# ScalarE's order within a chunk: evictions and side work ahead of the rounding of the chunk three ahead

## The chip, the cores and the metric

One NeuronCore of a Trainium2 chip runs the whole program. The metric is the device time of one execution in microseconds (us), less is better. The engines are TensorE (PE, its weight loads PEld), VectorE (DVE), ScalarE (ACT), GpSimd (POOL) and SyncE (SP), which issues nearly all DMAs. Each runs its own instructions in order and waits on semaphores for the others.

## The reference, cut to what matters

The reference chains two transformer blocks over 256 tokens of width 2048, all in float32. Nearly all its arithmetic is `x @ w` with a token matrix of 256 rows:

```python
# block 1
shift, scale, gate = split(silu(c) @ w_ada + b_ada, 3)        # and the same for the context
h = rmsnorm(x) * (1 + scale) + shift;   p = h @ w_in          # 2048 x 9216
attn = attention(rope(norm(q)), [k, kc], [v, vc])             # 12 query heads, 4 key heads
y = (sigmoid(g_a) * ((attn * silu(z_a)) @ w_proj_a)
     + sigmoid(g_b) * ((fourier_mix(u_b) * silu(z_b)) @ w_proj_b)) @ w_out
x = rmsnorm(x + gate * y) * final_g
# block 2
u = rms(x) * (1 + scale1) + shift1;     proj = u @ w_in_2     # 2048 x 18432
o_a = stick_breaking_attention(q, k, v)                       # 16 heads
o_b = gated_delta_rule(conv(q), conv(k), conv(v), g, beta)    # 16 heads, chunks
x = x + gate1 * ((sigmoid(ga) * (o_a @ p_a) + sigmoid(gb) * (o_b @ p_b)) @ w_out_2)
x = x + gate2 * ((silu(u2 @ w_gate) * (u2 @ w_up)) @ w_down)  # u2 from x as u, width 5632
```

## The kernel before, in words

**Stripes and chunks.** Every large weight matrix is read once, in stripes of 512 output columns. A stripe is a series of chunks; a chunk is 256 rows of weights (two tiles of 128x512, 512 KB) and is loaded by one DMA into a ring `raw` of six slots. There are 936 chunks in one fixed order, `of_chunk`; a chunk's number is called its beat. The phases come in the order ada with ctx and the first of in1 between, in1, ab1, out1, in2, pb2, ab2, out2, ffa, dna, ffb, dnb.

**Two roundings.** A float32 product is made of three passes in the format fp32r. For chunk n, ScalarE writes the rounded weights `w_hi` (`split_hi`, L411), then VectorE writes the rest `w_lo = raw - w_hi` (`split_lo`, L421). Both have three slots (`HL = 3`). TensorE then does eight matmuls of 128x512 on `w_hi` (L675) and four on `w_lo` (L681); in the ada phase it is two and two with a 4 column operand (L661, L665). Eight ada chunks need no rounding. The slot of chunk n + 3 is free when TensorE is done with chunk n, so both roundings of n + 3 wait for that. VectorE's `split_lo(n + 3)` also waits for ScalarE's `split_hi(n + 3)`.

**One beat of each engine.** Everything that isn't the stream of chunks is a side task, cut into steps by generators (`Track`, `yield k` gives the beat of the next step). TensorE at beat b: the matmuls of chunk b, then its side steps of b. VectorE at beat b: what the end of a stripe asks for, its side steps, `split_lo(b + 3)`, then a part of a matrix-vector product by hand (`macc`, L710). ScalarE at beat b: `split_hi(b + 3)`, then what the end of a stripe asks for, then its side steps. SP at beat b: the load of chunk b + 6 (after both roundings of chunk b), the load for L710, the store of a stripe that ended three beats earlier, its side steps. At two beats (starts of in2 and ffa) a hook follows: the normalisation of the rows.

**What ScalarE does at the end of a stripe.** A "store" stripe: it copies one half of the result from PSUM to `ost` (L560; VectorE the other half, L580), after an earlier store from that buffer has landed. A "rows" stripe (out1, out2): `square_rows`, sums of squares (L473, L480) of what VectorE's `add_rows` (L455, L458, L460 or L462) has just written. A "gate" stripe: a sigmoid. An "ada" stripe: the copy of a 4x512 row (L864), for which TensorE's L872 waits one beat later.

**Side steps of ScalarE that the text speaks of.** `first_squares` (L998), `stage_act` (L854) and `prep_act` (L899) at the start; squares of the attention heads (L1190) and the copy L1216; `gdn_act` (L1648, L1665, L1668, L1688 and others); `ba_act` (L1396); `sb_act` (three steps in one beat, L1971, L1973, L1975, for which VectorE's L1937 waits two beats later); `merge_sig_act` (L753), which waits for a DMA. TensorE's side steps that wait: L872, L523 (transposes of the normalised rows, behind VectorE's L508), L1556 (behind VectorE's L1753), L2007 (behind ScalarE's L1978) and L2015 (behind VectorE's L1950).

Of the kernel before, what the change touches and what calls it, by code (L numbers as in the profile page):

```python
# [49 lines left out]
HL = 3  # L50
# [87 lines left out]
def program(nc, a, y_out, dram):  # L138
    ctx = ExitStack()
    with ctx:  # L140
# [152 lines left out]
        def plain(st, kc):  # L293

            return st.phase == "ada" and kc == 4
        P0 = len(of_chunk)
        of_chunk += whole(S[3:])
        CHUNKS = len(of_chunk)
# [15 lines left out]
        def wait(eng, sem, value):  # L314
            if value > 0:
                eng.wait_ge(sem, value)
# [25 lines left out]
        for j, (base, step) in enumerate(mod_from):  # L342
            base = max(base, max(sum_at, default=-1) + 1)
            for k in range(MC):
                beat = base + (3 * step * (k // 2)) // 2 + k % 2
# [53 lines left out]
        def split_slot(n):  # L399

            k = halved[n]
            return k % HL, last_in[k - HL] + 1 if k >= HL else 0

        def split_hi(act, n):
            if plain(*of_chunk[n]):
                return
            use, slot = divmod(n, RAW)
            to, before = split_slot(n)
            act.wait_ge(s[f"raw{slot}"], 16 * (use + 1))
            wait(act, s["pe"], before)  # L410
            nc.scalar.copy(w_hi[:, to], raw[:, slot]).then_inc(s["hi"], 1)  # L411
# [23 lines left out]
        def evac(eng, st, m, copy, sem):  # L435

            eng.wait_ge(s["pe"], st.end)
            staging(eng, st)
            copy(ost[:, st.slot, m], bank(st.bank + m)).then_inc(s[sem], 1)
# [24 lines left out]
        def square_rows(act, st):  # L464

            cols = slice(st.o * W, (st.o + 1) * W)
            k = st.res - 1
            if st.phase == "out1":
                act.wait_ge(s["res_x"], st.res)
                for m in range(M):  # L470

                    wait(act, s["sq"], 4 * k + m)
                    nc.scalar.activation(sq_junk, ost[:, st.slot, m], ACT.Square,  # L473
                                         accum_out=nss[:, 0, m, st.o:st.o + 1]).then_inc(s["sq"], 1)
            if st.phase != "dnb":
                act.wait_ge(s["res"], st.res)
                done = 4 * k + 2 if st.phase == "out1" else 16 + 2 * (k - 4)
                for m in range(M):
                    act.wait_ge(s["sq"], done + m)
                    nc.scalar.activation(sq_junk, E[:, m, cols], ACT.Square,  # L480
                                         accum_out=nss[:, 1, m, st.o:st.o + 1]).then_inc(s["sq"], 1)
# [68 lines left out]
        def stream_act(act, items, hooks):  # L550
            sides = [Track(act, l) for l in items]
            for n in range(HL):
                split_hi(act, n)
            for beat in range(CHUNKS):
                if beat + HL < CHUNKS:
                    split_hi(act, beat + HL)
                st = ends.get(beat)
                if st is not None:
                    if st.kind == "store":
                        evac(act, st, 0, lambda dst, src: nc.scalar.copy(dst, src), "ev_act")  # L560
                    elif st.kind == "rows":
                        square_rows(act, st)
                    elif st.kind == "gate":
                        ff_gate_act(act, st)
                    elif st.kind == "ada":
                        ada_row_act(act, st)
                for side in sides:
                    side.run(beat)
                if beat + 1 in hooks:
                    hooks[beat + 1](act)  # L570

# [142 lines left out]
        def ff_gate_act(act, st):  # L714
            act.wait_ge(s["pe"], st.end)

            wait(act, s["ff_ev"], 2 * st.f)
            nc.scalar.activation(ff_sig, pair(st.bank), ACT.Sigmoid).then_inc(s["ff_sig"], 1)
# [142 lines left out]
        def ada_row_act(act, st):  # L861
            act.wait_ge(s["pe"], st.end)
            wait(act, s["ad_col"], st.idx - 1)
            nc.scalar.copy(ada_row[:, st.idx % 2], ada_out(st.idx)).then_inc(s["ad_row"], 1)  # L864
# [1236 lines left out]
        def _(act):  # L2101
# [55 lines left out]
            items += [(FFB, norm_rest, 1), (FFB + 5, h2_stored, 0)]  # L2157
            turns = [(st.n0, merge_sig_act, st) for st in MERGES] + [(st.done + 1, ep_act, st) for st in TURNS]
            stream_act(act, [first, preps, gates, items, sorted(turns, key=lambda item: item[0])], {B: norm_x1, FFB: norm_h2})

        @block.vector
# [211 lines left out]
```

## Time and profile before

| | |
|---|---|
| runs | 2927.20, 2916.00, 2926.41 us, median 2926.41 |
| profiled execution, its own time | 2926.73 us |
| its span, first to last instruction | 2924.8 us (1.9 us lie around it) |
| PE busy | 2838.9 us, 97% |
| PEld busy | 2328.3 us, 80% |
| DVE busy | 2024.5 us, 69% |
| ACT busy | 1348.3 us, 46% |
| DMA | 709.71 MB, mean 243 GB/s |
| mean granted TensorE clock | 0.987 |

How to read it: a row of a timeline is start, duration, engine and line, operation, output<-inputs, shapes, count; in brackets the idle time of the engine just before and what ended it. A row without brackets followed its predecessor without idle time. TensorE's granted clock has two levels, 1.2 GHz (0.5) and 2.4 GHz (1.0).

### The profile page before, as it was taken

What the parts mean: (1) busy time and instruction counts of PE and PEld (TensorE: products, weight loads), DVE (VectorE), ACT (ScalarE), POOL (GpSimd) and SP (SyncE); (2) the same over time, 40 slices, a digit from 0 to 9 for tenths busy, and PEclk for the clock granted to TensorE, in tenths of its full rate; (3) what the DMA queues carried; (4) which work ended last, traced back from release to release, by engine and by line L of the source; (5) the groups of instructions that cost most, each with busy time, mean ns of one, the idle gap of its engine ahead of it and who ended that gap; (6) DMA issues with size and microseconds to landing.
All of it is one profiled execution on the core that took longest, in us unless ns stands there. A gap on an engine that the chain in (4) does not pass through costs nothing.

```text
span 2924.8 us, 37083 instructions
## 1 busy us (share of the span) xinstructions
PE 2838.9 (97%) x13703; PEld 2328.3 (80%) x13703; DVE 2024.5 (69%) x2413; ACT 1348.3 (46%) x1725; POOL 73.3 (3%) x49
## 2 busy tenths in 40 slices
PE   7899999999989999999999999999999999999999
PEld 3468888778777888888888788887878888888877
DVE  6678777768776777777775788775657765445554
ACT  6544444444463535354544555554454444444433
POOL 0000000000000101000000000000000000000000
PEclk9999999999999999999999999999999999999999
DMA  8888777869758665656556788877757775665664
GB/s 311 283 321 325 259 251 240 278 219 343 279 207 318 208 217 181 216 169 218 173 180 233 266 288 295 307 251 251 254 192 257 281 249 190 214 201 190 197 243 151
DMA packets 223475, 709.71 MB, mean 243 GB/s; under 512 B 26768, under 2 KB 42432, under 8 KB 220480
## 3 DMA queue, kind: packets, MB, share of 16 engines
q1 hardware_dynamic: 222144, 703.04, 69.5%
q0 software_dynamic: 576, 4.19, 0.3%
q8 instruction: 109, 1.79, 0.3%
q14 instruction: 70, 0.57, 0.1%
q10 hardware_dynamic: 576, 0.11, 0.0%
HBM read 663.20 MB, written 44.06 MB: 242 GB/s over the span
## 4 chain that ended last, share of the span: by engine, by line
PE 86%; DVE 5%; DMA 3%; issue 3%; ACT 2%; POOL 1%; SPq 0%; DVEq 0%; ACTq 0%
PE ps L675 48%; PE ps L681 24%; DVE w_lo L421 2%; PE ps L1602 1%; PE ps L1592 1%; DMA mraw<-in_w_mod 1%; DVE macc L710 1%; ACT w_hi L411 1%; PE ps L1256 1%; PE ps L1241 1%; PE ps L1596 1%; PE ps L788 1%; DMA E<-in_ctx 1%; POOL arena L1819 1%; PE ps L665 0%
## 5 line engine op out<-in xcount | busy, mean ns | idle before, releaser
L411 ACT CAST w_hi<-raw 128x1024 fp32r<-128x1024 f32 x928 | 971.2, 1049 | 1443.4 <-PE ps L681 1397.7
L421 DVE TENSOR_TENSOR w_lo<-raw,w_hi 128x1024 fp32r<-128x1024 f32 x928 | 1127.6, 1221 | 548.9 <-ACT w_hi L411 544.9
L675 PE MATMUL ps<-w_hi,hT_hi 128*128 128x512 f32 x2688 | 749.1, 401 | 8.3 <-ACT w_hi L411 5.4
L681 PE MATMUL ps<-w_lo,hT_hi 128*128 128x512 f32 x2688 | 721.4, 390 | 5.7 <-DVE w_lo L421 5.7
L675 PE MATMUL ps<-w_hi,hT_lo 128*128 128x512 f32 x2688 | 721.6, 390 | 0.0
L681 PEld LDWEIGHTS ps<-w_lo,hT_hi 128*128 128x128 f32 x2688 | 505.6, 188 | 113.4 <-DVE w_lo L421 7.4
L675 PEld LDWEIGHTS ps<-w_hi,hT_lo 128*128 128x128 f32 x2688 | 506.4, 188 | 107.6
L675 PEld LDWEIGHTS ps<-w_hi,hT_hi 128*128 128x128 f32 x2688 | 490.9, 189 | 106.5 <-issue 14.4
L710 DVE SCALAR_TENSOR_TENSOR macc<-mraw,silu_c,macc 128x512 f32<-128x512 f32 x420 | 314.5, 749 | 20.0 <-DMA mraw<-in_w_mod 12.1
L681 PE MATMUL ps<-w_lo,fT_hi 128*128 128x512 f32 x800 | 215.3, 391 | 3.7 <-DVE w_lo L421 3.7
L675 PE MATMUL ps<-w_hi,fT_hi 128*128 128x512 f32 x800 | 217.9, 394 | 0.0
L675 PE MATMUL ps<-w_hi,fT_lo 128*128 128x512 f32 x800 | 215.6, 392 | 0.0
L681 PEld LDWEIGHTS ps<-w_lo,fT_hi 128*128 128x128 f32 x800 | 151.2, 189 | 35.8 <-DVE w_lo L421 4.2
L675 PEld LDWEIGHTS ps<-w_hi,fT_lo 128*128 128x128 f32 x800 | 151.3, 189 | 31.9
L675 PEld LDWEIGHTS ps<-w_hi,fT_hi 128*128 128x128 f32 x800 | 149.2, 189 | 30.3
L580 DVE COPY ost<-ps 128x512 f32<-128x512 f32 x64 | 44.0, 687 | 27.0 <-PE ps L681 21.3
L1719 DVE SCALAR_TENSOR_TENSOR arena<-ps,arena 128x255 f32<-128x255 f32 (+2 forms) x144 | 59.1, 471 | 0.2 <-ACT arena L1640 0.2
L1795 DVE TENSOR_TENSOR arena<-arena,ps 128x1024 f32<-128x1024 f32 x24 | 29.3, 1221 | 40.0 <-PE ps L1602 40.0
L661 PE MATMUL ps<-w_hi,sT 128*4 128x512 f32 x112 | 40.0, 442 | 9.7 <-ACT w_hi L411 9.7
L1592 PEld LDWEIGHTS ps<-arena 128*128 128x128 f32 x384 | 46.5, 191 | 1.9
L1602 PEld LDWEIGHTS ps<-arena 128*128 128x128 f32 x384 | 46.5, 191 | 1.9
L665 PE MATMUL ps<-w_lo,sT 128*4 128x512 f32 x112 | 39.0, 433 | 8.1 <-DVE w_lo L421 7.4
(300 smaller groups left out, 1779.5 us busy)
## 6 DMA issues: line engine op xcount, KB each, us to landing
raw<-in_w_in SPq DMA_DIRECT2D x432, 512.0 KB, 4.7
mraw<-in_w_mod SPq DMA_DIRECT2D x192, 512.0 KB, 4.2
raw<-in_w_gate SPq DMA_DIRECT2D x88, 512.0 KB, 4.2
raw<-in_w_up SPq DMA_DIRECT2D x88, 512.0 KB, 4.3
raw<-in_w_down SPq DMA_DIRECT2D x88, 512.0 KB, 4.3
raw<-in_w_ada SPq DMA_DIRECT2D x64, 512.0 KB, 5.5
raw<-in_w_out SPq DMA_DIRECT2D x64, 512.0 KB, 4.5
scratch_p<-ost SPq DMA_DIRECT2D x54, 512.0 KB, 5.3
```

Source lines behind the costliest of these rows:

```text
L411: nc.scalar.copy(w_hi[:, to], raw[:, slot]).then_inc(s["hi"], 1)
L421: nc.vector.tensor_tensor(w_lo[:, to], raw[:, slot], w_hi[:, to].bitcast(F32), ALU.subtract).then_inc(s["lo"], 1)
L580: evac(dve, st, 1, lambda dst, src: nc.vector.tensor_copy(dst, src), "ev_dve")
L661: pe.matmul(ada_out(st.idx), sT[:, kc * CK + t], w_hi[:, slot, t], start=(kc == 0 and t == 0), stop=False)
L665: mm = pe.matmul(ada_out(st.idx), sT[:, kc * CK + t], w_lo[:, slot, t], start=False, stop=(kc == st.chunks - 1 and t == CK - 1))
L675: pe.matmul(bank(st.bank + m), x, w_hi[:, slot, t], start=(kc == 0 and t == 0 and xp == 0), stop=False)
L681: mm = pe.matmul(bank(st.bank + m), x, w_lo[:, slot, t], start=False, stop=(kc == st.chunks - 1 and t == CK - 1))
L710: ins = nc.vector.scalar_tensor_tensor(macc[:], mraw[:, mk % 2, t], col, macc[:], ALU.mult, ALU.add)
L1592: mm = pe.matmul(tiles(4)[:, t], gL[:, t], gXT[:, t], start=True, stop=True)
L1602: mm = pe.matmul(tiles(4)[:, t], gX[:, t], gR[:, t], start=True, stop=True)
L1719: ins = vec.scalar_tensor_tensor(y, x, cw[:, k, h, 3 - j:4 - j], y, ALU.mult, ALU.add)
L1795: GV.done(vec.tensor_tensor(gXT, gXT, tiles(4), ALU.subtract), f"xt{lv}")
```

## The change

ScalarE's `split_hi(beat + HL)` is issued behind the stripe's end work and the side steps of the beat, ahead of the hook, no longer at the head of the beat. The instructions are the same ones, and no other engine's order is touched.

```diff
             for beat in range(CHUNKS):
-                if beat + HL < CHUNKS:
-                    split_hi(act, beat + HL)
                 st = ends.get(beat)
                 if st is not None:
                     if st.kind == "store":
...
                         ada_row_act(act, st)
                 for side in sides:
                     side.run(beat)
+                if beat + HL < CHUNKS:
+                    split_hi(act, beat + HL)
                 if beat + 1 in hooks:
                     hooks[beat + 1](act)
```

## Rows read from the trace of the kernel before

**Rows 1.** The page, section 1 (busy us, share of the span, instructions) and section 5.

```profile
PE 2838.9 (97%) x13703; PEld 2328.3 (80%) x13703; DVE 2024.5 (69%) x2413; ACT 1348.3 (46%) x1725; POOL 73.3 (3%) x49
...
L411 ACT CAST w_hi<-raw 128x1024 fp32r<-128x1024 f32 x928 | 971.2, 1049 | 1443.4 <-PE ps L681 1397.7
```

**Rows 2.** Waits of TensorE: for whom, us in total, times, longest.

```profile
PE ps L872 <- ACT aff L864: 15.1, 6, 4.7
...
PE ps L523 <- DVE E L508: 14.3, 2, 8.2
...
PE ps L1556 <- DVE arena L1753: 3.4, 4, 1.3
```

**Rows 3.** Timeline, one plain beat of ScalarE and VectorE.

```profile
836.39 1.05 ACT L411 CAST w_hi<-raw 128x1024 fp32r<-128x1024 f32 x1 [1.67 <-PE ps L681]
...
837.47 1.23 DVE L421 TENSOR_TENSOR w_lo<-raw,w_hi 128x1024 fp32r<-128x1024 f32 x1 [1.49 <-ACT w_hi L411]
```

**Rows 4.** Timeline of the ada phase, one row copy.

```profile
132.19 0.63 PE L665 MATMUL ps<-w_lo,sT 128*4 128x512 f32 x2
...
134.63 1.04 ACT L411 CAST w_hi<-raw 128x1024 fp32r<-128x1024 f32 x1 [2.47 <-DMA raw<-in_w_ada]
...
135.58 0.57 ACT L864 COPY aff<-ps 4x512 f32<-4x512 f32 x1
...
136.40 1.83 PE L872 MATMUL ps<-stat,aff 4*128 4x2 f32 x8 [3.58 <-ACT aff L864]
```

**Rows 5.** Timeline of the ada phase, one preparation of operands.

```profile
96.15 1.22 DVE L421 TENSOR_TENSOR w_lo<-raw,w_hi 128x1024 fp32r<-128x1024 f32 x1
...
96.27 1.14 ACT L899 CAST hT_hi<-arena 128x512 fp32r<-128x512 f32 x2 [0.34 <-DVE arena L889]
```

**Rows 6.** Timeline of the delta rule's first turn.

```profile
998.59 1.06 ACT L1648 ACTIVATE arena<-arena 128x1024 f32<-128x1024 f32 x1
...
999.68 1.23 DVE L1725 TENSOR_TENSOR arena<-arena 128x1024 f32<-128x1024 f32 x1 [2.45 <-ACT arena L1648]
...
1010.62 1.06 PE L1556 MATMUL ps<-c_ident,arena 128*128 128x128 f32 x8 [1.31 <-DVE arena L1753]
```

**Rows 7.** Timeline at the normalisation that opens in2.

```profile
842.72 1.22 DVE L421 TENSOR_TENSOR w_lo<-raw,w_hi 128x1024 fp32r<-128x1024 f32 x1
...
844.65 0.17 DVE L487 TENSOR_REDUCE nms<-nss 128x4 f32<-128x16 f32 x1 [0.71 <-ACT aff L480]
```

**Rows 8.** Timeline at the end of out1's third stripe.

```profile
816.85 1.05 ACT L411 CAST w_hi<-raw 128x1024 fp32r<-128x1024 f32 x1 [1.67 <-PE ps L681]
...
822.04 1.07 PE L675 MATMUL ps<-w_hi,hT_hi 128*128 128x512 f32 x4
...
823.27 2.94 ACT L411 CAST w_hi<-raw 128x1024 fp32r<-128x1024 f32 x3
```

**Rows 9.** Waits of ScalarE for DMAs: us in total, times, longest.

```profile
ACT E L753 <- DMA E<-scratch_p: 5.5, 1, 5.5
...
ACT b_two L1396 <- DMA arena<-in_w_ba: 5.4, 1, 5.4
...
ACT ost L560 <- DMA scratch_pc<-ost: 4.4, 1, 4.4
```

**Rows 10.** Timeline of TensorE at the start of ab2.

```profile
2001.60 2.05 PE L675 MATMUL ps<-w_hi,hT_hi 128*128 128x512 f32 x4 [2.80 <-ACT w_hi L411]
```

**Rows 11.** Stretch (us): busy PE, PEld, DVE, ACT, POOL; granted clock; DMA share; GB/s.

```profile
1990.00:2010.00 20.00, 17.20 (x69) 13.80 (x68) 8.19 (x7) 9.14 (x8) 0.00 (x0) 0.91 0.72 254
```

**Rows 12.** Timeline of a stick-breaking turn, ScalarE and VectorE.

```profile
1810.27 0.85 ACT L1971 ACTIVATE arena<-arena 128x768 f32<-128x768 f32 x1
...
1812.78 1.03 ACT L411 CAST w_hi<-raw 128x1024 fp32r<-128x1024 f32 x1
...
1813.85 1.22 DVE L421 TENSOR_TENSOR w_lo<-raw,w_hi 128x1024 fp32r<-128x1024 f32 x1 [2.47 <-ACT w_hi L411]
...
1816.44 0.95 DVE L1937 SCALAR_TENSOR_TENSOR arena<-arena 128x768 f32<-128x768 f32 x1
```

## Prediction

> **What bounds the kernel now.** I read the page first. TensorE is busy for 2838.9 of 2924.8 us, while the rounding on ScalarE leaves 1443.4 us of idle time in front of its 928 instances [rows 1]. So TensorE sets the time, and the change can win only from the 86 us in which TensorE stands still. The view of TensorE's waits says on what it stands: 15.1 us in six waits on the row copy L864, 14.3 us in two waits on the row normalisation, 3.4 us in four waits on VectorE's L1753, and smaller ones [rows 2]. No line of it names L560 or L580, the evictions. A stripe's banks are wanted again eight chunks later.
>
> Then the timelines. In a plain beat ScalarE is idle for 1.67 us until TensorE is done with chunk b, rounds chunk b + 3 in 1.05 us, and VectorE follows with 1.23 us [rows 3]. TensorE needs the rounded chunk only after two more chunks: rounding started at 816.85, its first matmul at 822.04 [rows 8]. That is 5.19 us, of which 4.14 us are slack (the rest is the rounding itself). This slack is the cover of the change. It hides any side task on ScalarE below about 4 us, and does not hide those that wait longer, nor those where VectorE's next task is itself on the path. For VectorE rounds chunk b + 3 behind ScalarE, in order, and all its later work stands behind that.
>
> **The change, part by part.** Nothing is added or removed; 928 roundings of 1.05 us move behind the side work of their beat. Two things follow. (a) Side work no longer waits for the raw chunk's DMA or for TensorE's chunk b, and starts 0.95 to 2.7 us earlier where its own inputs are there. (b) The rounding of b + 3, and with it VectorE's rounding and its next side task, wait for whatever ScalarE's side work waits for. SP's loads wait for both roundings of a chunk three beats old and have room; ScalarE issues no DMA in these beats.
>
> *Evictions.* 64 copies start 0.95 us earlier, worth 0: no wait of TensorE names them [rows 2]. The Trainium skill (PSUM — Partial Sum Buffer, Summary: rules for kernel authors) says to evacuate promptly, as the space is tight; by that rule the evictions alone would bring time, by the rows nothing.
>
> *Row copies in the ada phase (gain).* TensorE was done with chunk 60 at 132.8 (132.19 + 0.63), but the rounding ahead of the copy waited for a DMA until 134.63, and the copy came at 135.58; TensorE stood for 3.58 us [rows 4]. The copy now comes at 132.2, so about 3.5 us go. The same working on the other waits on L864 gives 2.1, 1.2, 0.5 and 1.8, and 0 for the first, where ScalarE itself is late. Together 9.1; the bounds are 2 (loads become the limit: DMA engines were 83% busy there) and 11.
>
> *Preparation of operands in the ada phase (loss).* L899 waits for VectorE (0.34 us idle before 96.27) and ends at 97.4; VectorE rounded at 96.15 [rows 5]. The rounding by ScalarE now ends at 98.4, so VectorE is held for 2.2 us on a stretch where it is the bound. Three such: 1.7 + 2.2 + 2.2 = 6.1; bounds 2 and 8. The fourth lies under full-length chunks and is hidden.
>
> *Attention turns and Fourier part (gain).* Squares L1190 and the copy L1216 start up to 2.7 us earlier; the small stalls of TensorE that hang on them sum to 2.3. Bounds 0 and 3.
>
> *Delta rule (gain).* L1648 stood behind the rounding, and VectorE idled for 2.45 us for it; TensorE later waited 1.31 us for the end of that chain [rows 6]. L1648's inputs are there one beat earlier, so VectorE gains more than 1.3 us, and all four waits (3.4 us [rows 2]) go. Bounds 0 and 3.4. In the solver's beats ScalarE's copy waits for TensorE, but there the side matmuls lengthen the slack to some 10 us: 0.
>
> *Normalisation, twice (loss).* VectorE rounded at 842.72 while ScalarE summed squares, and its statistics began when the squares were done, at 844.65 [rows 7]. Now ScalarE rounds only from 844.6 to 845.7, VectorE rounds behind it until 846.9, and the statistics begin 2.25 us later, with TensorE waiting for them already. Two places: 4.5. Bounds 4 and 6.
>
> *out1 (loss).* In the third stripe's last beat the squares of ScalarE ended at 823.3, and TensorE wanted the chunk at 822.04 [rows 8]. The rounding now ends at 824.4: 2.4 us of a stall that wasn't there. The second stripe gives 1.4 by the same sum. The first ends in a DMA delay; there the rounding would move from 769.2 behind squares that end at 777.5, and TensorE's twelve matmuls cost 3.5 more after its present stall. Sum 7.3; bounds 3 and 11.
>
> *Waits for DMAs on ScalarE (loss).* L753 waited 5.5 us at the start of ab2, L560 4.4 us once, L1396 5.4 us [rows 9]. Behind the first, TensorE already stalled for 2.80 us [rows 10]; one more chunk is now behind it, 2.8 us. Behind the second the slack of 4.14 is spent: 1.6. Behind the third VectorE is held, but earlier work there came 1.35 sooner: 0.9. Sum 5.3; bounds 2 and 9.
>
> *Stick-breaking turns (loss, the largest).* L1971, L1973 and L1975 follow one another from 1810.27 to 1812.8, all in one beat, and start when VectorE's input is there, not because of the rounding. After them ScalarE rounded for the next beat, and VectorE, idle for 2.47 us, rounded at 1813.85 and reached L1937 2.59 us later [rows 12]. Now two roundings stand behind L1975, ending 1813.85 and 1814.9; VectorE's second one begins at 1815.1, and L1937 at 1817.7 instead of 1816.44: 1.3 us, on a chain without idle time up to TensorE's next side matmuls. The same rows of the eight turns give 2.3, 0.9, 0, 0.8, 1.3, 0.7, 0, 0: 6.0. Bounds 0 (VectorE's other work gives way) and 10.
>
> *The first turn's start* gains 0.5, attention's first, with a table load, loses 0.3.
>
> *TensorE's clock.* After the stall at 2001.60 four matmuls took 2.05 us instead of 1.07 [rows 8, 10], and the granted clock of that stretch was 0.91 on average [rows 11]: part of it ran at 1.2 GHz. A stretch at that level costs about 1.6 us. New stalls of 2 us and more (out1, stick-breaking, the stored copy) buy some, the vanished ones of the ada phase give some back: +3, bounds -2 and +8.
>
> *Sum:* gains 9.1 + 2.3 + 3.4 + 0.5 = 15.3; losses 6.1 + 4.5 + 7.3 + 5.3 + 6.0 + 0.3 = 29.5; clock 3. Net +17.2 on 2926.7 of the profiled execution, which lies 0.3 above the median of 2926.4: 2943.6 and, against the median, 2943.
>
> **The skill's rule on waits.** The rows say that 15.1 us of TensorE's idle time are put down to ScalarE's row copy [rows 2]. The Trainium skill (Perfetto Trace Analysis, Optimization Strategies) says that when the matmul engine waits for other engines, the work that blocks the path is to be made faster. By it the change is right and the time some 15 us shorter; it counts what ScalarE hands to TensorE sooner, not the hand-over that is put off in exchange.
>
> **The rivals.**
>
> *The gains alone stay (faster).* The place is VectorE: if it has other work to do while its rounding is held, and TensorE's slack of 4.14 us covers the rest, only the gains remain: 2926.4 - 15.3 = 2911. It decides at the point where held-up work is below 4.14 us everywhere. For it: 69% of VectorE is busy, so there is other work. Against it: its queue is in order, so other work can't step in, and five places exceed the slack in the rows above.
>
> *Both cancel (no change).* The stick-breaking chain and the ada preparations are estimates from two engines' order. If VectorE catches up before TensorE's side matmuls (-6), and the DMA waits fall out shorter than in the one profiled execution (-3), the sum is +8: 2934.
>
> *Held loads (much slower).* Where the rounding is held for 8 us (out1's first stripe, ab2) the slots of `raw` come free later, SP waits in order, and the load of the by-hand product and of the next chunks bunch behind one another. Each of the two would cost another 5 to 10 us, with more time at 1.2 GHz: 2958. For it: that place already is a DMA delay. Against it: slots of `raw` are freed by chunks three beats older, which are long rounded.
>
> **Chances.** The forecast (slower, around 2943) 0.52; both cancel 0.34; faster 0.04; held loads 0.10. What a measurement can tell from no change is about 0.5%, 14.6 us: slower means above 2941. Of the forecast's 0.52 some 0.10 fall below that bound, so slower gets 0.42 + 0.10 = 0.52; within gets 0.34 + 0.10 = 0.44; faster 0.04. The range of 8 in 10 runs from 2928 (most of "both cancel") to 2958.
>
> **What would show it right or wrong.** In the profile of the changed kernel TensorE's waits on L864 should fall from 15.1 to about 6, and those on L1753 vanish. The waits on VectorE's L508 should grow from 14.3 to about 19. New waits of TensorE on w_hi should stand in out1, near the start of ab2 and near 200 us; those on L1950 and L1978 should grow by about 6 in the stick-breaking turns. ScalarE's idle time in front of L753, L473 and L1971 should stand ahead of the rounding. The prediction is wrong if TensorE's waits don't grow in sum by some 14 us, if VectorE rounds in the normalisation beat before the statistics without idling, or if the time changes by more than 35 us, which no row here would explain.

## The result and the profile after

The changed kernel took 2952.35 us (median of 4 runs, 2945.91 to 2953.07), the kernel before on the same chip 2924.56 us (4 runs). The ratio is 1.0099, with a 95% interval from 1.0083 to 1.0116: 29 us more (24 to 34). The prediction was 2943, with 2928 to 2958 as its range. Direction and range were right; the loss is 12 us larger than the sum said.

The page of the changed kernel, sections 1 and 5 (its span is 2951.1 us, before 2924.8):

```profile
PE 2844.8 (96%) x13703; PEld 2327.6 (79%) x13703; DVE 2026.4 (69%) x2413; ACT 1345.2 (46%) x1725; POOL 80.2 (3%) x49
...
L411 ACT CAST w_hi<-raw 128x1024 fp32r<-128x1024 f32 x928 | 967.8, 1049 | 953.3 <-PE ps L681 918.2
```

ScalarE's idle time ahead of the rounding fell from 1443.4 us [rows 1] to 953.3, since part of its waiting now stands ahead of other work. The span is 26.3 us longer. Of that, 5.9 us are busy time of TensorE with the same 13703 instructions (2844.8 less 2838.9), which goes with a mean granted clock of 0.983 where it was 0.987, and 20.4 us are idle time (106.3 less 85.9). In the changed kernel the eviction L560 is L558.

The waits of TensorE: for whom, us in total, times, longest. After:

```profile
PE ps L675 <- ACT w_hi L411: 23.5, 6, 12.2
PE ps L523 <- DVE E L508: 18.5, 2, 10.2
PE ps L661 <- ACT w_hi L411: 16.1, 7, 6.5
PE ps L665 <- DVE w_lo L421: 14.1, 18, 1.8
PE ps L2007 <- ACT arena L1978: 6.5, 4, 2.0
PE ps L690 <- DVE macc L710: 4.4, 2, 2.8
...
PE ps L681 <- DVE w_lo L421: 3.2, 5, 2.4
...
PE ps L872 <- ACT aff L864: 2.0, 1, 2.0
...
PE ps L1556 <- DVE arena L1725: 0.8, 3, 0.3
```

And the rows of before for the same matmuls that weren't shown above:

```profile
PE ps L661 <- ACT w_hi L411: 9.7, 3, 6.5
PE ps L681 <- DVE w_lo L421: 9.4, 5, 4.4
PE ps L665 <- DVE w_lo L421: 7.4, 8, 1.7
PE ps L675 <- ACT w_hi L411: 5.4, 2, 2.8
...
PE ps L2007 <- ACT arena L1978: 2.3, 2, 1.4
```

The exchange can be read line by line. The waits on the row copy fell from 15.1 us [rows 2] to 2.0 and those on L1753 are gone (0.8 us on L1725 stand in their place). The waits on rounded chunks grew: L675 by 18.1, L661 by 6.4, L665 by 6.7 us; only those of L681 on the rest `w_lo` fell, by 6.2; 4.4 of these are one wait in out1 that went into the 12.2 us of L675. The two normalisations took 4.2 us more (14.3 [rows 2] to 18.5), the exponential L1978 4.2.

Where the time came in, as the difference (after less before) of the starts of the same chunk's first matmul (below: the chunks' shift). The last column is the same step in those kernels of the experiments below that leave the stretch as it was (8 to 10 for each row):

| at (time before) | what lies behind it | after less before, us | step | step where nothing was changed |
|---|---|---|---|---|
| 169 | ada phase | +3.5 | +3.5 | -4.9 to +1.9 |
| 607 | in1, attention, Fourier part | +2.5 | -1.0 | -0.6 to +1.8 |
| 855 | ab1, out1, first normalisation | +16.1 | +13.6 | -1.2 to +1.4 |
| 911 | start of in2 | +19.0 | +2.9 | -2.7 to +0.3 |
| 1616 | delta rule | +16.3 | -2.7 | 0.0 |
| 1643 | start of the first stick-breaking turn | +14.1 | -2.2 | -1.5 to +0.1 |
| 1960 | eight stick-breaking turns | +26.4 | +12.3 | 0.0 to +0.8 |
| 2187 | ab2, out2, second normalisation | +28.6 | +2.2 | -4.6 to +0.1 |
| 2916 | feed-forward part | +26.3 | -2.3 | -2.4 to +0.1 |

So two profiles show what out1, the delta rule and the stick-breaking turns cost or give, and say little of the ada phase and of ab2. The last step isn't the change's: it is a wait at 2839 us, 3.75 us before and 2.39 after, with the clock behind it, which shrank by as much in experiments that leave this part alone (2.50 in one, 2.31 in another). Now the places, with the rows of after that answer to those of before.

*Row copy and preparation in the ada phase* (answers to [rows 4, 5]):

```profile
98.46 1.14 ACT L899 CAST fT_hi<-mraw 128x512 fp32r<-128x512 f32 x2 [1.74 <-DVE mraw L889]
...
103.00 1.23 DVE L421 TENSOR_TENSOR w_lo<-raw,w_hi 128x1024 fp32r<-128x1024 f32 x1 [2.15 <-ACT w_hi L411]
...
138.82 1.05 PE L872 MATMUL ps<-stat,aff 4*128 4x2 f32 x8
```

The matmul behind the row copy starts without idle time, where it had waited 3.58 us. In exchange ScalarE waits 1.74 us for VectorE's L889 with its rounding behind it, and VectorE then waits 2.15 us for that rounding: the two engines take turns waiting for one another.

*out1 and the first normalisation* (answers to [rows 7, 8]):

```profile
782.43 2.04 PE L675 MATMUL ps<-w_hi,hT_hi 128*128 128x512 f32 x4 [12.16 <-ACT w_hi L411]
...
832.58 2.93 ACT L411 CAST w_hi<-raw 128x1024 fp32r<-128x1024 f32 x3
...
833.75 1.17 PE L675 MATMUL ps<-w_hi,hT_hi 128*128 128x512 f32 x4 [2.68 <-ACT w_hi L411]
...
857.37 1.23 DVE L421 TENSOR_TENSOR w_lo<-raw,w_hi 128x1024 fp32r<-128x1024 f32 x1 [2.79 <-ACT w_hi L411]
858.51 0.16 DVE L487 TENSOR_REDUCE nms<-nss 128x4 f32<-128x16 f32 x1
...
861.03 3.68 PE L523 MATMUL ps<-c_ident,E 128*128 128x128 f32 x16 [10.22 <-DVE E L508]
```

In the third stripe the three roundings stand in one block behind the squares, and TensorE waits 2.68 us where it had waited for nothing. At the normalisation VectorE's rounding stands right ahead of the statistics L487: they wait for it, and it waited 2.79 us for ScalarE's rounding, which now stands behind the squares. TensorE's wait L523 grew from 8.15 to 10.22 us.

*A stick-breaking turn*, the one of [rows 12]:

```profile
1835.58 0.85 ACT L1975 ACTIVATE arena<-arena 128x768 f32<-128x768 f32 x1
1836.33 2.94 ACT L411 CAST w_hi<-raw 128x1024 fp32r<-128x1024 f32 x3
...
1837.39 2.36 DVE L421 TENSOR_TENSOR w_lo<-raw,w_hi 128x1024 fp32r<-128x1024 f32 x2 [3.60 <-ACT w_hi L411]
...
1841.12 0.95 DVE L1937 SCALAR_TENSOR_TENSOR arena<-arena 128x768 f32<-128x768 f32 x1
...
1847.48 0.84 ACT L1978 ACTIVATE arena<-arena 128x768 f32<-128x768 f32 x1 [5.89 <-DVE arena L1947]
...
1848.38 0.87 PE L2007 MATMUL ps<-c_ident,arena 128*128 128x128 f32 x6 [1.98 <-ACT arena L1978]
```

From the end of ScalarE's three steps (1835.58 + 0.85) to L1937 it is now 4.69 us; before it was 3.56 us (1812.88 to 1816.44). VectorE's idle time ahead of its rounding grew from 2.47 to 3.60.

### The profile page after: what moved, and what is told of

Read it like the earlier page. It is cut to its first block, busy times and chain, and to the rows that moved or that the text cites. A ratio compares the mean times of both kernels' runs of the same rounds, so it can differ in the third digit from the quotient of the medians.

```text
span 2951.1 us, 37082 instructions
## 1 busy us (share of the span) xinstructions
PE 2844.8 (96%) x13703; PEld 2327.6 (79%) x13703; DVE 2026.4 (69%) x2413; ACT 1345.2 (46%) x1725; POOL 80.2 (3%) x49
## 3 DMA queue, kind: packets, MB, share of 16 engines
q8 instruction: 109, 1.79, 0.2%
## 4 chain that ended last, share of the span: by engine, by line
PE 84%; DVE 6%; issue 3%; ACT 3%; DMA 3%; SPq 0%; POOL 0%; DVEq 0%; ACTq 0%
PE ps L675 48%; PE ps L681 24%; DVE w_lo L421 2%; PE ps L1592 1%; PE ps L1602 1%; ACT w_hi L411 1%; DVE macc L710 1%; DVE arena L1719 1%; PE ps L1256 1%; PE ps L1241 1%; DMA mraw<-in_w_mod 1%; PE ps L1596 1%; PE ps L788 1%; DMA raw<-in_w_ada 1%; PE ps L690 0%
## 5 line engine op out<-in xcount | busy, mean ns | idle before, releaser
L411 ACT CAST w_hi<-raw 128x1024 fp32r<-128x1024 f32 x928 | 967.8, 1049 | 953.3 <-PE ps L681 918.2
L675 PE MATMUL ps<-w_hi,hT_hi 128*128 128x512 f32 x2688 | 751.0, 401 | 25.6 <-ACT w_hi L411 23.5
L681 PE MATMUL ps<-w_lo,hT_hi 128*128 128x512 f32 x2688 | 721.6, 390 | 0.8 <-DVE w_lo L421 0.8
L675 PE MATMUL ps<-w_hi,hT_lo 128*128 128x512 f32 x2688 | 721.7, 390 | 0.0
L675 PEld LDWEIGHTS ps<-w_hi,hT_lo 128*128 128x128 f32 x2688 | 506.6, 188 | 107.8
L681 PEld LDWEIGHTS ps<-w_lo,hT_hi 128*128 128x128 f32 x2688 | 505.9, 188 | 108.6 <-DVE w_lo L421 2.5
L675 PEld LDWEIGHTS ps<-w_hi,hT_hi 128*128 128x128 f32 x2688 | 490.9, 189 | 126.2 <-issue 29.3
L710 DVE SCALAR_TENSOR_TENSOR macc<-mraw,silu_c,macc 128x512 f32<-128x512 f32 x420 | 314.5, 749 | 21.2 <-DMA mraw<-in_w_mod 13.1
L675 PE MATMUL ps<-w_hi,fT_hi 128*128 128x512 f32 x800 | 219.1, 396 | 0.0
L681 PE MATMUL ps<-w_lo,fT_hi 128*128 128x512 f32 x800 | 215.1, 391 | 2.4 <-DVE w_lo L421 2.4
L675 PE MATMUL ps<-w_hi,fT_lo 128*128 128x512 f32 x800 | 216.1, 392 | 0.0
L681 PEld LDWEIGHTS ps<-w_lo,fT_hi 128*128 128x128 f32 x800 | 150.8, 189 | 34.4 <-DVE w_lo L421 2.8
L675 PEld LDWEIGHTS ps<-w_hi,fT_lo 128*128 128x128 f32 x800 | 151.9, 190 | 32.2
L675 PEld LDWEIGHTS ps<-w_hi,fT_hi 128*128 128x128 f32 x800 | 149.9, 190 | 31.0 <-issue 0.6
L558 ACT COPY ost<-ps 128x512 f32<-128x512 f32 x64 | 37.6, 587 | 97.4 <-PE ps L681 90.7
L1688 ACT COPY arena<-ps 128x1024 f32<-128x1024 f32 x20 | 20.4, 1019 | 118.4 <-PE ps L1596 118.4
L661 PE MATMUL ps<-w_hi,sT 128*4 128x512 f32 x112 | 39.2, 434 | 16.1 <-ACT w_hi L411 16.1
L665 PE MATMUL ps<-w_lo,sT 128*4 128x512 f32 x112 | 39.5, 438 | 14.7 <-DVE w_lo L421 14.1
L1602 PEld LDWEIGHTS ps<-arena 128*128 128x128 f32 x384 | 46.5, 191 | 1.9
```

The costliest lines, as they stand in the source:

```text
L661: pe.matmul(ada_out(st.idx), sT[:, kc * CK + t], w_hi[:, slot, t], start=(kc == 0 and t == 0), stop=False)
L665: mm = pe.matmul(ada_out(st.idx), sT[:, kc * CK + t], w_lo[:, slot, t], start=False, stop=(kc == st.chunks - 1 and t == CK - 1))
L675: pe.matmul(bank(st.bank + m), x, w_hi[:, slot, t], start=(kc == 0 and t == 0 and xp == 0), stop=False)
L681: mm = pe.matmul(bank(st.bank + m), x, w_lo[:, slot, t], start=False, stop=(kc == st.chunks - 1 and t == CK - 1))
L710: ins = nc.vector.scalar_tensor_tensor(macc[:], mraw[:, mk % 2, t], col, macc[:], ALU.mult, ALU.add)
L1602: mm = pe.matmul(tiles(4)[:, t], gX[:, t], gR[:, t], start=True, stop=True)
```

## The experiments

All use one edit of the kernel before, which puts the rounding in one of three places of ScalarE's beat. `at` is 0 for the head (as before), 1 for behind the stripe's end work, 2 for behind everything (as in the change); the experiments differ in the line that sets it.

```diff
             for beat in range(CHUNKS):
-                if beat + HL < CHUNKS:
+                at = ...
+                if beat + HL < CHUNKS and at == 0:
                     split_hi(act, beat + HL)
...
+                if beat + HL < CHUNKS and at == 1:
+                    split_hi(act, beat + HL)
                 for side in sides:
                     side.run(beat)
+                if beat + HL < CHUNKS and at == 2:
+                    split_hi(act, beat + HL)
```

The theory was that the loss is made in a few beats, in which ScalarE waits with a rounding queued behind it and either TensorE lacks the chunk or VectorE is held behind its own rounding. The rival was a loss spread over all beats, evictions or the clock. Times are in us against the kernel before measured beside each (the recorded ratio less 1, times its median; 95% interval in brackets). Plain differences of the medians lie up to 2 us away. In the experiments the lines behind the edit stand 5 lower than in the kernel before: L877 is L872, L680 is L675, L1942 is L1937. In the two kernels of the last pair all lines from L411 on stand 4 lower.

**The ada phase alone.**

```diff
+                at = 2 if beat < P0 else 0
```

> The rounding stands behind ScalarE's other work only in the beats of the ada phase; everywhere else as before. My theory (a rounding held behind side work costs, a row copy freed from it gains): by the comparison of the two traces the ada phase ends 3.5 us later in the changed kernel, so +3.5 us, with the preparations of operands losing about 10 and the row copies giving back some 7; the prediction's own terms say 6.1 - 9.1 = -3.0. The rival (the loss of the whole change is spread evenly, some generic lateness of each beat or of the clock) would give the phase its share of the span, 169/2927 of 27, that is +1.5, with no place in it standing out.

Measured: +3.2 (0.9 to 5.8). The sign is the theory's and not that of the prediction's own terms (-3.0); the rival's 1.5 lies within the interval, so this run alone doesn't decide. Its profile doesn't help: there the phase ended 1.6 us earlier than in the profile of before, and unchanged phases scatter by more than that (table above).

**The ends of the row stripes alone.**

```diff
+                at = 2 if beat in ends and ends[beat].kind == "rows" else 0
```

> The rounding stands behind ScalarE's other work only in beats that end a stripe of rows (out1, the two row normalisations), some 20 of 928. My theory: these few beats carry about half of the loss; by the traces +9 to +10 for out1 and +4.4 to +5 for the normalisations, so +12 to +15 us (the prediction's terms: 7.3 + 4.5 = 11.8). The rival (every beat contributes the same) gives 20/928 of 27, that is +0.6.

Measured: +12.3 (9.1 to 15.8), and TensorE's waits are those of the changed kernel: L523 18.5 us in two, the longest wait on w_hi 11.9 us. These are twelve beats (fewer than the expectation has), and they carry two fifths of the loss. The spread-out rival can't give that.

**One beat of each stick-breaking turn.**

```diff
+                at = 2 if beat - 7 in SB_AT else 0
```

> The rounding stands behind ScalarE's other work in eight beats alone, those in which the three operations L1971 to L1975 of a stick-breaking turn run. My theory, in its sharp form: +6 us as the prediction summed it; the trace of the changed kernel is 12.3 us later over these turns, so if these eight beats carry all of it, +12; anything between says how much of the 12.3 comes from other beats of the turns (squares and the z - x step). The rival gives 0.2.

Measured: +6.7 (4.1 to 9.3). In the same turn as above VectorE reads as in the changed kernel:

```profile
1815.31 2.36 DVE L421 TENSOR_TENSOR w_lo<-raw,w_hi 128x1024 fp32r<-128x1024 f32 x2 [3.61 <-ACT w_hi L411]
...
1819.04 0.95 DVE L1942 SCALAR_TENSOR_TENSOR arena<-arena 128x768 f32<-128x768 f32 x1
```

So the predicted term (6.0) was right for the beat it spoke of, and the rest of the loss over these turns is made elsewhere. TensorE's waits on the exponential rose to 6.1 us (2.3 before) by this beat alone.

**The row copies' gain alone.**

```diff
+                at = 1 if beat in ends and ends[beat].kind == "ada" else 0
```

> The rounding stands behind the row copy L864 in the last beats of the ada stripes, but ahead of the preparations and all other side work. My theory: the row copies' gain without the preparations' loss, -9.1 us by the prediction's term (bounds -2 and -11). The rival (the loads are the limit in the ada phase, so an earlier row only moves the wait to the DMA): -2 or less.

Measured: -5.0 (-7.6 to -2.6). The waits of TensorE say why it isn't 9.1 (the row copy, w_lo, w_hi in the ada phase):

```profile
PE ps L670 <- DVE w_lo L421: 10.4, 11, 1.5
PE ps L666 <- ACT w_hi L411: 10.1, 4, 6.5
...
PE ps L877 <- ACT aff L869: 5.8, 2, 3.7
```

The wait on the copy fell by 9.3 us, from 15.1 to 5.8, as predicted. Of that 3.0 came back as waits on w_lo (7.4 to 10.4) and 0.4 on w_hi: the next chunk was late too, and had been hidden behind the copy. (In kernels that leave the phase alone the wait on the copy is 13.0 to 14.9 us, so the fall may be 2 us smaller.) The ada phase alone cost +3.2, so 3.2 + 5.0 = 8.2 us are left for the preparations, give or take some 3.5 by the two intervals.

**The other beats of the stick-breaking turns.**

```diff
+                at = 2 if any(beat - k in SB_AT for k in (0, 5, 11, 13)) else 0
```

> The rounding stands behind ScalarE's other work in the remaining beats of the stick-breaking turns alone: 0, 5, 11 and 13 beats after a turn's start (squares, the copy L1963, the exponential L1978, the last copy). The three operations of beat 7, which alone cost 6.7 us, stand as before. The two traces are 12.3 us apart over these turns, so what my sum left out would be here: +5.6 us, with TensorE's waits on L1978 of about 2 us in turns 0 and 1. By the prediction's own sum (only beat 7 costs) and by the generic rival it is 0.

Measured: +2.9 (0.6 to 5.6), not 0 and not 5.6. In the turn at 1825 us the exponential waited 5.19 us for VectorE with two roundings behind it. TensorE waited 1.79 us for it and then again, for VectorE's copy of the result (0.19 us in the kernel before), which stood behind the second of these roundings:

```profile
1829.88 1.35 PE L2020 MATMUL ps<-arena 128*128 128x128 f32 x10 [0.99 <-DVE arena L1955]
```

**All beats of the turns.**

```diff
+                at = 2 if SB_AT[0] <= beat < SB_AT[-1] + 14 else 0
```

> The change in all beats of the stick-breaking turns and in no other. Beat 7 alone cost 6.7 us, the other four kinds of beat 2.9. If the costs add, 9.6; if two held roundings of one turn meet in one chain, as the traces of the whole change suggest, +12.3 us.

Measured: +13.7 (10.2 to 17.2), against 6.7 + 2.9 = 9.6 for the parts. With the uncertainty of the two parts the intervals allow a plain sum. The traces say more. Over the turns (1643 to 1960 us) the kernel with the one beat lost 8.4 us, the one with the other beats 3.1, in sum 11.5; the changed kernel lost 12.3, which a plain sum explains within the 0.8 us by which unchanged turns differ, and this kernel 14.3. The 2.0 us between the last two are mostly one place (1.2 us). Here a wait of 2.83 us on VectorE's L710 was followed by four matmuls at half speed (2.06 us); the changed kernel's wait there, 2.80 us at 1796.94, was not (1.17 us for the first four). The same wait was 1.54 us with the one beat alone and absent with the others alone.

```profile
1782.27 1.12 PE L695 MATMUL ps<-c_ident,macc 128*128 128x128 f32 x4 [2.83 <-DVE macc L715]
1783.04 2.06 PE L680 MATMUL ps<-w_hi,hT_hi 128*128 128x512 f32 x4
```

**The three beats with DMA waits.**

```diff
+                at = 2 if beat in (87, 301, 609) else 0
```

> The rounding stands behind ScalarE's other work in three beats alone, those in which ScalarE waits for a DMA: L560 near 202 us, L1396 near 900 us, L753 near 1999 us. The prediction's terms: 1.6 + 0.9 + 2.8 = +5.3. The differences of the two traces at the three places: 1.0 + 2.9 + 1.9 = +5.8, so my theory says +5 to +6. The rival (each of these DMAs lands when it lands, and the slack of two chunks covers it) says 0 to +1.

Measured: +7.3 (4.7 to 10.2). The wait at the start of ab2 is 4.53 us instead of 2.80 [rows 10], and the next matmuls ran at the lower level in both; TensorE's wait behind L1396 is 3.7 us instead of 2.8. By the chunks' shift the three places cost 0.5, 2.1 and 2.5 us, 5.1 in sum, where the prediction had 1.6, 0.9 and 2.8.

```profile
2003.57 2.04 PE L680 MATMUL ps<-w_hi,hT_hi 128*128 128x512 f32 x4 [4.53 <-ACT w_hi L411]
```

**Is it VectorE that is held in the normalisation?** Both norm beats as in the change, but VectorE's rounding goes behind the statistics:

```diff
+                at = 2 if beat + 1 in hooks else 0
...
-                if beat + HL < CHUNKS:
+                if beat + HL < CHUNKS and beat + 1 not in hooks:
                     split_lo(dve, beat + HL)
...
                 norm_stat_dve(dve, 0)
+                split_lo(dve, B - 1 + HL)
...
                 norm_stat_dve(dve, 1)
+                split_lo(dve, FFB - 1 + HL)
```

> At the two normalisations alone the rounding stands behind the squares, as in the changed kernel, but VectorE's own rounding of that chunk is put behind the statistics of the norm (it was ahead of them), so that it no longer holds them. My theory (VectorE's next task is held behind its rounding): TensorE's waits at L523 return from 10.22 and 8.25 us to about 8.2 and 6.2, and the time is within 1 us of the kernel before. The rival (the rounding itself comes late, or the clock costs): the waits stay near 10.2 and 8.2 and the time is +4.

```profile
844.77 0.17 DVE L487 TENSOR_REDUCE nms<-nss 128x4 f32<-128x16 f32 x1 [1.85 <-ACT aff L480]
...
845.70 1.22 DVE L421 TENSOR_TENSOR w_lo<-raw,w_hi 128x1024 fp32r<-128x1024 f32 x1 [0.16 <-ACT w_hi L411]
```

```profile
PE ps L523 <- DVE E L508: 15.7, 2, 8.6
```

The statistics start at 844.77, as in the kernel before (844.65 [rows 7]), although ScalarE rounds behind the squares. The two waits sum to 15.7 us, against 18.5 in the change and 14.3 before; two thirds of the loss go, and what stays is VectorE's rounding, now between the statistics and the scaling L508. The time is +3.2 (0.6 to 5.6), more than the 1 us expected; the waits explain 1.4 of it, the rest is within the interval. The rival's +4 is within it too, so it is the waits that decide here, not the time.

**The gains alone.**

```diff
+                at = (2 if 91 <= beat < OUT1 or GD_AT[0] <= beat < GD_AT[-1] + 40
+                      else 1 if beat in ends and ends[beat].kind == "ada" else 0)
```

> The change only where I hold that it gains: behind the row copy L864 at the ends of the ada stripes (not behind the preparations), and behind everything in the beats of in1 and ab1 (attention, Fourier part) and of the delta rule. My theory: -5.0 (measured for the row copies) - 4.0 (attention, by the traces) - 2.7 (delta rule, by the traces) = -12 us, about 2910. The prediction's terms give -9.1 - 2.3 - 3.4 = -15. The rival (the gains are partly the clock or chance of one profile): -5 to -7.

Measured: 2910.71, -10.2 (-14.0 to -6.1). This kernel beats both the kernel before and the changed one.

**All that is left.**

```diff
+                at = (0 if beat in (87, 301, 609) or beat in ends and ends[beat].kind == "rows"
+                      or SB_AT[0] <= beat < SB_AT[-1] + 14
+                      else 2 if beat >= P0
+                      else 1 if beat in ends and ends[beat].kind == "ada" else 0)
```

> The changed kernel, but with the rounding ahead, as before, in the beats that I hold responsible for the loss: the preparations of the ada phase (only the row copy stays ahead of the rounding there), the ends of the row stripes, the three beats with DMA waits, and all beats of the stick-breaking turns; some 140 of 928. In all others, more than 740, the rounding stands behind the evictions and the other work. My theory (the list is complete and the rest of the change is free): the same as the kernel with the gains alone, -10 to -12 us against before, about 2911. The rival (something small is lost in each beat or each eviction): clearly above that, by its share of the loss +10 and more.

Measured: 2911.28, -10.8 (-14.6 to -7.3), the same as the gains alone. The several hundred further beats with the rounding behind evictions (13 of the 64) and feed-forward work cost and bring nothing that these intervals of 4 us either way would show, and the rival's +10 is excluded: the list of places is complete to that extent.

**The slack by itself.** Twelve plain beats of the feed-forward part in which ScalarE is held ahead of the rounding by copies into the same slot, three in one kernel and five in the other (5 in place of 3):

```diff
+            if 768 <= n - HL < 816 and n % 4 == 0:
+                for j in range(3):
+                    nc.scalar.copy(w_hi[:, to], raw[:, slot]).then_inc(s["jk"], 1)
+                    act.wait_ge(s["jk"], (n // 4 - 193) * 3 + j + 1)
             nc.scalar.copy(w_hi[:, to], raw[:, slot]).then_inc(s["hi"], 1)
```

> The kernel before, with ScalarE held for about 3.2 us ahead of its rounding in 12 plain beats (three copies of 1.05 us into the same slot, one after the other; nothing is left out). My theory (a plain chunk has 4.14 us of slack): 0 us, within 1.5. The rival (each held rounding passes on its delay, through VectorE or through the loads): 12 x 1 to 3 = +12 or more.

> As the kernel with three copies, with five: ScalarE is held for about 5.3 us in the same 12 beats. My theory: each costs the excess over the slack, 5.3 - 4.14 = 1.2 us, so +14 us, with 12 waits of TensorE on w_hi of 1.2 us each, and no more unless the clock falls. The rival (a delay is wholly passed on): 12 x 5.3 = +64. A slack greater than I read it: 0.

Three copies: +0.6 (-2.0 to 2.9), and no wait of TensorE in the whole stretch. Five: +18.1 (14.6 to 21.6), a little above the 14 expected. ScalarE, TensorE and the waits of the stretch from 2450 to 2620 us, with five copies (L413 the copies, L415 the rounding):

```profile
2469.73 5.37 ACT L413 CAST w_hi<-raw 128x1024 fp32r<-128x1024 f32 x5 [1.69 <-PE ps L685]
2475.13 2.95 ACT L415 CAST w_hi<-raw 128x1024 fp32r<-128x1024 f32 x3
```

```profile
2474.01 1.07 PE L685 MATMUL ps<-w_lo,fT_hi 128*128 128x512 f32 x4
2476.32 1.17 PE L679 MATMUL ps<-w_hi,fT_hi 128*128 128x512 f32 x4 [1.25 <-ACT w_hi L415]
2477.33 1.08 PE L679 MATMUL ps<-w_hi,fT_lo 128*128 128x512 f32 x4
```

```profile
PE ps L679 <- ACT w_hi L415: 14.0, 12, 1.2
```

The rounding starts 5.40 us late (2475.13 less 2469.73) and TensorE waits 1.2 us, twelve times. This bears out the slack of 4.14 us that the prediction read from one pair of rows: 3.2 us of holding are free, and 5.40 make TensorE wait for the excess. Each hold moves the later chunks by 1.53 us, a little more than the wait that the trace shows, which is why the twelve cost 18 us and not 14.

## Why the prediction was right, and where it was short

| step | predicted | measured | by |
|---|---|---|---|
| row copies | -9.1 | -5.0 | row copies alone |
| preparations | +6.1 | +8.2 | ada phase less row copies |
| attention (-2.3, +0.3 for its first), delta rule (-3.4) | -5.4 | -5.2 | gains alone less row copies |
| out1 and both normalisations | +11.8 | +12.3 | row stripes alone |
| DMA waits | +5.3 | +7.3 | three beats alone |
| stick-breaking turns (+6.0), start of the first (-0.5) | +5.5 | +13.7 | all beats of the turns |
| clock | +3 | in the others | |
| sum | +17.2 | +31.3, whole change +29 | |

The sum is applied with a slip of half a microsecond: 17.2 on 2926.7 is 2943.9, and 2943.6 against the median of 2926.4, where the text has 2943.6 and 2943. It changes nothing.

**The signs that it named.** TensorE's waits grew by 20.5 us in sum (79.3 to 99.8), where at least 14 were asked for. L864 fell to 2.0, further than the 6 forecast, L1753 vanished, L508 rose to 18.5 (forecast 19). New waits on w_hi stand at 207 and 250 us, in out1 and at the start of ab2. L1950 and L1978 grew by 4.4 us together, for 6 forecast, and L710 by 2.9, which wasn't forecast.

**The mechanism** stands. The sum of the separately measured parts, 31 us, agrees with the whole, within the whole's interval of 24 to 34; its own uncertainty, from the intervals of the six kernels behind it, is some 8 us. Rows that differ from the prediction by 1 or 2 us can't be told from it. The rounding's slack of about 4 us hides most of what was put ahead of it, and the loss sits at the named places. *The gains alone stay* failed on its condition, and as a kernel in its own right it gave 2911, the figure that the rival had. *Held loads* is refuted as a price: out1's first stripe cost 4.9 us by the chunks' shift, not 5 to 10 on top of 3.5, and its wait of 12.16 us answers to 6.99 us in the kernel before:

```profile
770.43 1.16 PE L675 MATMUL ps<-w_hi,hT_hi 128*128 128x512 f32 x4 [2.61 <-ACT w_hi L411]
...
776.90 2.08 PE L681 MATMUL ps<-w_lo,hT_hi 128*128 128x512 f32 x4 [4.38 <-DVE w_lo L421]
```

*Both cancel* needed shorter DMA waits and a VectorE that catches up; neither came.

**out1 and the normalisations** came out near their terms. Each of the norm's two waits grew by 2.07 us where 2.25 was worked out. The three stripes of out1 cost 4.9, 1.5 and 2.9 us in the chunks' shift, where the sum had 3.5, 1.4 and 2.4. The step of +13.6 us in the table holds 2.3 us more, which are clock (below).

**The stick-breaking turns are the term that was too small**, 6.0 us against 13.7 (12.3 in the trace of the changed kernel). The sum counted one beat of each turn, and that beat alone costs 6.7 us, for 6.0 predicted. It took ScalarE's other steps of the turn (the copy behind TensorE's transposes, the exponential, the last copy) as covered. They are not: the exponential waits up to 5.9 us for VectorE's L1947, two roundings stand behind it, VectorE's next copy waits for the second, and TensorE for the copy. These beats alone cost 2.9 us. That the two kinds cost more together than apart is not shown: the traces have 11.5 us for the parts and 12.3 for the changed kernel, and the kernel with all beats lost its further 2 us mostly where the lower clock followed one wait.

**The row copies were read from the wait alone.** The term was 9.1 us, the time fell by 5.0 (2.6 to 7.6). The wait fell by the predicted amount, and 3.4 us of it came back in TensorE's next waits, on w_lo and w_hi of the following chunks. The Trainium skill (Perfetto Trace Analysis, Optimization Strategies) has the right sign for this single step; the prediction's reading of it, that the whole wait of 15 us is gained, is three times what the kernel with the row copies alone brought. The Trainium skill's other rule weighed in the prediction, prompt eviction (PSUM — Partial Sum Buffer, Summary: rules for kernel authors), shows no effect here: no wait of TensorE names an eviction before or after, and the kernel with all that is left, in which 13 more of the 64 evictions come ahead of the rounding, is no faster than the one with the gains alone. No run moved the evictions by themselves.

**The DMA waits** cost 7.3 us (4.7 to 10.2), so the 5.3 of the sum isn't excluded. Seen from ScalarE they grew: the first holds a chunk behind 6.6 us (L558) instead of 4.4 [rows 9], and L753 and L1396 likewise wait longer, since ScalarE reaches them without its wait for TensorE and its rounding ahead of them:

```profile
ACT E L753 <- DMA E<-scratch_p: 8.4, 2, 6.9
...
ACT b_two L1396 <- DMA arena<-in_w_ba: 7.8, 1, 7.8
ACT ost L558 <- DMA scratch_pc<-ost: 6.6, 1, 6.6
```

**The clock.** TensorE's busy time grew by 5.9 us where the sum had 3. Of the 5.9, 2.3 lie behind the first normalisation: the first matmuls there took 1.15 us before and 2.05 in the changed kernel, half speed. But the kernel with the three DMA beats, which leaves this place alone, has the same (2.04 us) and lost 2.3 us by it. So this part can't be put down to the change, and what the term for the clock should have been stays open. The rows are of before, after and the three DMA beats:

```profile
851.76 1.15 PE L675 MATMUL ps<-w_hi,hT_hi 128*128 128x512 f32 x4 [0.92 <-DVE hT_lo L547]
```

```profile
865.62 2.05 PE L675 MATMUL ps<-w_hi,hT_hi 128*128 128x512 f32 x4 [0.92 <-DVE hT_lo L547]
```

```profile
850.21 2.04 PE L680 MATMUL ps<-w_hi,hT_hi 128*128 128x512 f32 x4 [0.92 <-DVE hT_lo L547]
```

Open is the ada phase's size. Eight experiments leave this phase as it was, and by its end their single profiles lie 4.9 us ahead to 1.9 us behind that of the kernel before. A comparison of two profiles tells nothing below that there; the medians of the runs were needed.

## What to carry to other kernels

When an in-order engine feeds a pipelined one, ask of every instruction moved ahead of the feeding step how long it can wait itself, not how long it runs, and compare with the slack of the hand-over, which one held beat measures. Follow the hold one engine further: the rounding was rarely late for TensorE, but VectorE's next task, queued behind its own half of the rounding, often was. A move that gains in some places and loses in others is worth making by place: the same two lines moved in the right beats gave 2911 us, everywhere 2952. And measure how far the profiles of an unchanged stretch differ before reading a difference of two profiles as the change's.

## What the runs showed of the hardware

Waits of TensorE of nearly the same length were followed by different clocks. After 2.00 us at 1720.82 the next four matmuls took 1.98 us, half speed; after 1.98 us at 1848.38 they took 1.17. The waits of 2.83 and 2.80 us above show the same, and so do the normalisation's waits of 8.2 us in the kernel before and in the one with the three DMA beats (1.15 and 2.04 us behind them), so the length of a wait alone doesn't tell the clock behind it. And a wait costs more than its idle time, even where the clock stays up. The twelve waits of 1.2 us left it at 1.00 throughout (last row), yet moved the chunks by 1.53 us each. By the starts of the rows above, 2474.01 and 2476.32 lie 2.31 apart where such groups lie 0.91 apart, so 1.40 are lost there, and the next start, 2477.33, is another 0.10 late. Part of this is how idle time is counted: a group is shown as 1.07 us long though the next one follows after 0.91, and the idle time of 1.25 us counts from its end.

```profile
1720.82 1.54 PE L2007 MATMUL ps<-c_ident,arena 128*128 128x128 f32 x6 [2.00 <-ACT arena L1978]
1722.01 1.98 PE L675 MATMUL ps<-w_hi,hT_hi 128*128 128x512 f32 x4
```

```profile
2465.00:2610.00 145.00, 130.62 (x562) 104.74 (x563) 59.70 (x53) 107.28 (x107) 0.00 (x0) 1.00 0.55 184
```
